# Eight vector additions and six rotation passes change engine, and one loop body is taken out of a TensorE loop

## The reference, cut to what matters

```python
hc = modulate(rms_norm_2(ctx, norm1_g[l]), m_ctx[0], m_ctx[1])   # needs sum(ctx*ctx) over 2048 features
...
qa = apply_rope(qa, cos_a, sin_a)     # x*cos + swapped(x)*sin
ka = apply_rope(ka, cos_a, sin_a)
qb = apply_rope(qb, cos_b, sin_b)
kb = apply_rope(kb, cos_b, sin_b)
...
merged = jax.nn.sigmoid(g_a) * (o_a @ w_br_a) + jax.nn.sigmoid(g_b) * (o_b @ w_br_b)
```

## Time and profile before

| | |
|---|---|
| median of 3 runs | 2875.73 us (2875.54 to 2875.75) |
| the profiled execution, its own time | 2876.91 us |
| its span in the trace | 2875.1 us |
| PE busy | 2811.4 us (98%) |
| DVE busy | 1997.1 us (69%) |
| ACT busy | 1274.9 us (44%) |
| POOL busy | 86.0 us (3%) |
| granted TensorE clock, mean | 0.994 |

### The profile page before, as it was taken

How to read it: one execution, slowest core, us unless ns; L and a number is a source line. 1 busy time by engine, 2 the same in 40 slices (tenths; PEclk the granted TensorE clock), 3 DMA queues, 4 the chain that set the end, 5 groups by cost and what they waited for, 6 DMA issues and landing times.

```text
span 2875.1 us, 52879 instructions
## 1 busy us (share of the span) xinstructions
PE 2811.4 (98%) x19046; PEld 2575.8 (90%) x19046; DVE 1997.1 (69%) x3060; ACT 1274.9 (44%) x1587; POOL 86.0 (3%) x74
## 2 busy tenths in 40 slices
PE   8998899999999999999999999999989999999999
PEld 8998899998899988888889898899988888888888
DVE  6776789867799987666678667866665555555554
ACT  5344455544454444211344455654444444344443
POOL 0011000100000000000003100000000000000000
PEclk9999999999999999999999999999999999999999
DMA  8874678667888885577777655666656666666665
GB/s 306 273 246 126 214 264 275 192 181 247 258 265 273 275 269 174 178 239 241 263 228 246 209 168 159 211 186 181 183 154 185 188 186 187 188 184 187 186 188 163
DMA packets 211744, 612.77 MB, mean 213 GB/s; under 512 B 23472, under 2 KB 31792, under 8 KB 210992
## 3 DMA queue, kind: packets, MB, share of 16 engines
q1 hardware_dynamic: 199296, 591.49, 65.9%
q10 hardware_dynamic: 11008, 14.60, 1.6%
q0 software_dynamic: 1328, 5.24, 0.5%
HBM read 600.75 MB, written 5.77 MB: 211 GB/s over the span
## 4 chain that ended last, share of the span: by engine, by line
PE 88%; DVE 6%; issue 3%; DMA 2%; ACT 1%; DVEq 0%; SPq 0%; ACTq 0%
PE acc L1624 24%; PE acc L1620 24%; PE acc L1622 12%; PE acc L1623 12%; DMA cond_rows<-w_ada 2%; PE acc L1608 2%; PE acc L1610 2%; PE acc L1611 2%; PE sums L1823 1%; PE acc L1618 1%; DVE cond_rows L1170 1%; PE acc L1831 1%; DVE wlo L1027 1%; PE turned L1816 1%; PE acc L1617 1%
## 5 line engine op out<-in xcount | busy, mean ns | idle before, releaser
L1027 DVE TENSOR_TENSOR wlo<-raw,whi 128x1024 fp32r<-128x1024 f32 x864 | 1064.2, 1233 | 713.9 <-ACT whi L560 711.5
L560 ACT ACTIVATE whi<-raw 128x1024 fp32r<-128x1024 f32 x864 | 914.6, 1060 | 1363.0 <-PE acc L1624 1132.4
L1624 PE MATMUL acc<-operand,wlo 128*128 128x256 f32 (+1 forms) x4816 | 1396.3, 290 | 0.0
L1622 PE MATMUL acc<-operand,whi 128*128 128x256 f32 (+1 forms) x3136 | 925.7, 295 | 29.2 <-DVE wlo L1027 14.0
L1624 PEld LDWEIGHTS acc<-operand,wlo 128*128 128x128 f32 x4816 | 921.8, 191 | 14.6
L1623 PE MATMUL acc<-operand,whi 128*128 128x256 f32 (+1 forms) x3136 | 923.9, 295 | 0.0
L1622 PEld LDWEIGHTS acc<-operand,whi 128*128 128x128 f32 x3136 | 603.4, 192 | 43.7 <-issue 25.4
L1623 PEld LDWEIGHTS acc<-operand,whi 128*128 128x128 f32 x3136 | 603.4, 192 | 12.7
L1620 PE MATMUL acc<-operand,whi 128*128 128x512 f32 x1680 | 599.9, 400 | 6.1 <-DVE operand L1385 5.7
L1620 PE MATMUL acc<-ffn_act,whi 128*128 128x512 f32 x1344 | 472.0, 395 | 0.0
L1620 PEld LDWEIGHTS acc<-operand,whi 128*128 128x128 f32 x1680 | 316.7, 189 | 81.7 <-issue 6.8
(11 more groups left out here) (220 smaller groups left out, 2005.2 us busy)
## 6 DMA issues: line engine op xcount, KB each, us to landing
cond_rows<-w_ada SPq DMA_DIRECT2D x512, 256.0 KB, 4.3
raw<-w_in SPq DMA_DIRECT2D x224, 512.0 KB, 3.6
raw<-w_up SPq DMA_DIRECT2D x176, 512.0 KB, 4.5
raw<-w_down SPq DMA_DIRECT2D x88, 512.0 KB, 3.7
raw<-w_fg SPq DMA_DIRECT2D x88, 512.0 KB, 3.8
raw<-w_fu SPq DMA_DIRECT2D x88, 512.0 KB, 3.5
raw<-w_fd SPq DMA_DIRECT2D x88, 512.0 KB, 3.5
raw<-w_o SPq DMA_DIRECT2D x32, 512.0 KB, 3.8
```

The source lines that it names most:

```text
L560: act.activation(whi[j % RING][:], raw[j % RING][:], ACT.Copy).then_inc(hi_done, 1)
L1027: dve.tensor_tensor(wlo[j % RING][:], raw[j % RING][:], whi[j % RING][:].bitcast(F32), ALU.subtract).then_inc(lo_done, 1)
L1622: pe.matmul(out_, h[:, x, f], mov[:, 0], start=first, stop=False)
L1624: ins = pe.matmul(out_, l[:, x, f], mov[:, 0], start=False, stop=last)
```

## The change

- GpSimd's 8 additions of the context squares are removed; VectorE gets the same 8 additions as `add_squares(i)`, put at steps 1, 2, 5 and 6 of the first two bodies of `up1b`. These two bodies are written out, the other three stay in VectorE's loop. ScalarE and TensorE keep their code there.
- GpSimd's 6 rotation passes for chunks 10 and 11 are removed; VectorE gets them one pass at a time, chunk 10 at steps 48, 50 and 52, chunk 11 at steps 58, 60 and 62, each after the norm work of the step and before the attention work of the step. The waits of those who read the chunks change accordingly.
- TensorE's first body of `branch_a` is written out, with the wait for one more group and the wait for the operand; the remaining three stay in a loop with `fresh=False`, and so without these two waits.

```diff
+        ctx_added = sem("context_squares_added")
...
-        TURNS_A = {6: 1, 0: 2, 7: 3, 1: 4, 8: 5, 9: 6}
-        TURNS_B = {2: 1, 3: 2, 4: 3, 5: 4, 10: 5, 11: 6}
+        TURNS_A = {6: 1, 0: 2, 7: 3, 1: 4, 8: 5, 9: 6, 10: 7, 11: 8}
+        TURNS_B = {2: 1, 3: 2, 4: 3, 5: 4}
+        TURN_AT = {48: (10, 0), 50: (10, 1), 52: (10, 2), 58: (11, 0), 60: (11, 1), 62: (11, 2)}
...
-            pool.wait_ge(sq_ready, SQ[5][0])
-            n, turn = KT // 2, 0
-            while n:
-                pool.wait_ge(poolstep, count)
-                for k in range(0, n, 2):
-                    pool.wait_ge(hi_done, unit(st_up1b, turn // st_up1b.upb, turn % st_up1b.upb) + 1)
-                    turn += 1
-                    a, b = (XC32[:, x + k:x + min(k + 2, n), 1, 1, :] for x in (0, n))
-                    step(pool.tensor_tensor(a, a, b, ALU.add))
-                n //= 2
-            pool.wait_ge(poolstep, count)
-            pool.sem_inc(acc_ready, 1)
...
-            for c in (2, 3, 4, 5, 10, 11):
+            for c in (2, 3, 4, 5):
                 for i in range(3):
                     rotate_late(c, i)
...
                         act.wait_ge(a_out, HA)
-                        act.wait_ge(n_late, 18)
+                        act.wait_ge(n_rope, 8)
...
-            run(st_up1b)
+            sums = [(n, k, min(k + 2, n)) for n in (8, 4, 2, 1) for k in range(0, n, 2)]
+
+            def add_squares(i):
+
+                n, k0, k1 = sums[i]
+                dve.wait_ge(sq_ready, SQ[5][0])
+                if n < 8:
+                    dve.wait_ge(ctx_added, [x[0] for x in sums].index(n))
+                dst, src = (XC32[:, x + k0:x + k1, 1, 1, :] for x in (0, n))
+                dve.tensor_tensor(dst, dst, src, ALU.add).then_inc(acc_ready if n == 1 else ctx_added, 1)
+
+            for b in range(2):
+                body(st_up1b, b, then={at: lambda i=4 * b + x: add_squares(i) for x, at in enumerate((1, 2, 5, 6))})
+            with dve.Fori(2, st_up1b.bodies) as b:
+                body(st_up1b, b)
...
-            def rotate(c):
+            def rotate(c, parts=range(3)):
 
                 n = TURNS_A[c]
                 chunk, sw, dims = rotation(c)
                 cos, sin = table(c)
-                if c < NK:
-                    dve.wait_ge(k_swap[c % 2], swapped(c))
-                else:
-                    dve.wait_ge(q_swap[c % 2], swapped(c))
-                    dve.wait_ge(n_sq, job_of[c] + 1)
-                    dve.wait_ge(n_table, 2)
-                dve.tensor_tensor(chunk, chunk, rep(cos, *dims), ALU.mult).then_inc(n_t1, 1)
-                dve.tensor_tensor(sw, sw, rep(sin, *dims), ALU.mult).then_inc(n_t2, 1)
-                dve.wait_ge(n_t1, n)
-                dve.wait_ge(n_t2, n)
-                dve.tensor_tensor(chunk, chunk, sw, ALU.add).then_inc(n_rope, 1)
+                if 0 in parts:
+                    if c < NK:
+                        dve.wait_ge(k_swap[c % 2], swapped(c))
+                    else:
+                        dve.wait_ge(q_swap[c % 2], swapped(c))
+                        dve.wait_ge(n_sq, job_of[c] + 1)
+                        dve.wait_ge(n_table, 4)
+                    dve.tensor_tensor(chunk, chunk, rep(cos, *dims), ALU.mult).then_inc(n_t1, 1)
+                if 1 in parts:
+                    dve.tensor_tensor(sw, sw, rep(sin, *dims), ALU.mult).then_inc(n_t2, 1)
+                if 2 in parts:
+                    dve.wait_ge(n_t1, n)
+                    dve.wait_ge(n_t2, n)
+                    dve.tensor_tensor(chunk, chunk, sw, ALU.add).then_inc(n_rope, 1)
...
-                    if c in TURNS_A and c >= NK:
+                    if c in TURNS_A and NK <= c < 10:
                         rotate(c)
+                if s in TURN_AT:
+                    rotate(TURN_AT[s][0], TURN_AT[s][1:])
...
                     if n == 0:
-                        pe.wait_ge(n_late, 18)
+                        pe.wait_ge(n_late, 12)
+                        pe.wait_ge(n_rope, 8)
                     score_b(n)
...
-            run(st_ba)
+            body(st_ba, 0)
+            with pe.Fori(1, st_ba.bodies) as b:
+                body(st_ba, b, fresh=False)
```

More of the change, by code:

```diff
@@ L535, in rotate_late @@
                 if step == 0:
-                    if c < NK:
-                        pool.wait_ge(k_swap[c % 2], swapped(c))
-                    else:
-                        pool.wait_ge(q_swap[c % 2], swapped(c))
-                        pool.wait_ge(n_sq, job_of[c] + 1)
+                    pool.wait_ge(k_swap[c % 2], swapped(c))
                     ins = pool.tensor_tensor(chunk, chunk, rep(cos, *dims), ALU.mult)
```

## The result

The changed kernel took 2856.97 us (median of 4 runs, 2856.56 to 2857.5) against 2875.74 us before. The ratio is 0.9932 with a 95% interval of 0.9919 to 0.9944. Times the 2875.73 us that the prediction started from, this is 2856.2 us. In a second session the same kernel came out at a ratio of 0.9941 (0.9926 to 0.9956), which is 2858.8 us by the same count. The prediction was 2858.4 us, with a range from 2856.8 to 2865.0.

A forecast was written before the change was run, and what follows sets the result against it. PE, busy for 98% of the span, bounds the kernel, so apart from the clock only its idle time can be won. Gains of 6.4+7.1+3.75 = 17.3 us from 2875.73 give 2858.4 us, range 2856.8 to 2865.

The forecast's parts named there:

- The squares: Near 534 us, moving GpSimd's additions to VectorE removes PE's 4.67 us idle time and 1.76 of slow clock and restart: 6.4 us.
- the slack of 2.0 us: Near 534 us, without GpSimd's additions VectorE's low part is done at 532.2, before PE asks at 534.20.
- The bound of 0.9 for the gain: Lower bound of the squares' gain, 0.9 us, against 5.5 us of additions on the path if VectorE's waits hid none.
- The rotations: Ahead of attention A, moving chunks 10 and 11 to VectorE gains 7.1 us of 8.3, bounds 1.2 and 8.3.
- the chain from the first exponential: Attention A: the 4.52 us from the first exponential to PE's transposes stay.
- the second wait of 0.4 us: After attention A's first transposes, a second small PE wait of 0.4 us can come, subtracted from the rotations' gain.
- the ring's bound: Before attention A's transposes, ScalarE's ring limits the start, leaving PE idle 0.1 to 0.3 us; 0.8 was taken.
- The cover for chunk 10's passes: At steps 48, 50 and 52 VectorE's DMA waits (2.38 us) hide the passes; 3.7 us without that cover.
- Rival (A): Wait ahead of attention A largely remains: chunk 10's passes add 3.7 us, idle 5.4, time 2864.4; chance 0.17.
- Branch A: Dropping the evacuation wait from three later bodies of the stage gains 3 x 1.25 = 3.75 us.
- the range's low end: Whole kernel: 2857.0 us in the likeliest case, all 18.5 us won; 2856.8 in the stated range.
- Rival (D): Attention steps 58 to 62: chunk 11's passes make PE wait in each step, costing 25 us, time 2883; chance 0.03.

The follow-up runs named there:

- the burst: Changed kernel with all eight square additions on VectorE in a row, ahead of the low part PE asks for after 534 us; ratio to the kernel before 0.9948.
- the experiment with whole rotations: Changed kernel with chunk 10's three passes together at step 46 and chunk 11's together at step 54; ratio to the kernel before 0.9945.
- the squares alone: Kernel before with only the context squares' additions moved from GpSimd to VectorE; ratio to the kernel before 0.998.
- the additions spread: Kernel before with the additions still on GpSimd, one for every second unit from the stage's second body on; ratio to the kernel before 0.9977.

## Why the prediction was right, and where it was not

**The squares** (6.4 us predicted, 6.43 measured): the step from 11.80 us on POOL to a late low part, and the slack of 2.0 us (2.3 by the burst), hold. The price of 0 for the additions holds for where they stand: the addition at 540.59 took 0.60 us of VectorE's idle time and PE shows no wait. The bound of 0.9 for the gain, with the cover gone, was close to what the burst left, 6.43-5.88 = 0.55 us.

**The rotations** (7.1 us predicted, 7.33 alone and 7.51 in the changed kernel): the chain from the first exponential (4.52 us before, 1587.97 to 1592.49 here) and the second wait of 0.4 us (0.39) came as worked out. The idle time that I took as 0.8 us was 0.37, near the ring's bound, and that is the mis-sized term of the sum: 8.34-0.37-0.39 = 7.6 us. Ahead of the first maximum VectorE waits for ScalarE and PE. In the 25 us ahead of the first exponential, all four profiles with chunk 10 on GpSimd have waits for `w_ada` DMAs as in the earlier trace rows, the longest of 1.96 to 2.39 us, and none has them with its passes in pieces on VectorE. So they were an after-effect of the stall by chunk 10 and no limit of their own. The cover for chunk 10's passes, which the prediction took from these DMA waits, came from waits for ScalarE instead (0.92 us at 1578.09). Rival (A) is out in the form in which it was priced, but the experiment with whole rotations shows its mechanism: passes ahead of the first maximum come onto the path in full.

**Branch A** (3.75 us predicted, 3.75 and 3.73 measured).

**Contention.** The rule of the Trainium skill, SBUF — State Buffer, "Who interferes with whom", agrees with the traces here where it says that the two engines lock each other out: VectorE's instructions are long beside GpSimd, and GpSimd's additions take up to 2.33 us beside VectorE. It also says what the prediction left out, that a VectorE instruction in a two-port mode contends with GpSimd too. The scaling passes of up to 1.24 us have one tensor as input, and so has a cast that takes 0.43 us elsewhere and 1.27 us beside a spread addition:

```profile
547.68 1.76 POOL L519 TENSOR_TENSOR operand_scratch<-operand_scratch 128x512 f32<-128x512 f32 x1 [3.43 <-ACT whi L560]
548.47 1.27 DVE L1153 CAST ffn_act<-conv_out 128x512 f32 x1 [0.17 <-DVE conv_out L1149]
```

**The step that failed** is the range's low end, "2857.0 (all 18.5 us won)" (2875.73-18.5 is 2857.2). It put every place that no edit touches at nothing. The prediction had read the granted clock as "1.00 elsewhere", and that was wrong: in the kernel before the clock is 0.91 in 203 to 213 us and 0.66 in 2120 to 2130. The changed places gave 6.43+7.51+3.75 = 17.7 us in the first profile, and the span fell by 20.3. Of the rest, 1.72 us lie before 245.96 and 1.15 in the 24 us after 2105 (0.2 come back later), in code that is the same, with a granted clock that differs between two profiles of one kernel. The low end should have been some 2 us lower for these places alone. The prediction's own figure for what a measurement can tell, 5.8 us, also stood against a low end 1.6 us below its centre. That the centre was met within 2.2 us by one session (19.5 us won) and 0.4 by the other (17.0) is in part luck, since nothing in the sum decides where these places fall. The statement that idle times of 1.88 us leave the clock alone was too strong as well: in the kernel with the squares alone the same wait, before 1874.18, had a body of 25.79 us behind it, with a granted clock of 0.84 from 1876 to 1886:

```profile
1876.00:1886.00 10.00, 10.00 (x74) 10.00 (x73) 5.87 (x4) 6.94 (x9) 0.00 (x0) 0.84 0.42 112
```

Rival (D) didn't come: the attention steps from 58 to 62 show no idle time, with 0.84 us to spare in the tightest one that I read.

**Open:** why the clock falls or not at the same idle time isn't settled. In the first block's attention it goes with the start of the stretch, but no run moved that start alone. Nor was it tried whether more of the 0.76 us left ahead of attention A can be had.

## What to carry to other kernels

A busy engine's idle time is a short list. Read it whole, and ask of each row what ran elsewhere at that time: the engine named as the releaser (VectorE here) may be slow only because a third one (GpSimd) works beside it. Work that is nobody's bottleneck is dear in one piece ahead of a result with little slack, on either engine. The squares' additions cost nothing in pieces behind the urgent low part, on VectorE or on GpSimd, and the same work in one burst ahead of it gave back 5.88 of 6.43 us; the rotations in whole gave back 5.94 of 7.51. Before a range is closed, look at the places that the edit doesn't touch: here they alone moved a profile by up to 1.7 us each. A first body that needs a stricter wait than the others belongs outside the loop, since in the loop each of the others pays for it.

## What the runs showed of the hardware that I had not expected

- An idle time of 2.95 us of PE cost 5.88 us in all, and one of 4.67 us cost 6.43: the slow clock behind the shorter wait took more. The idle time alone doesn't tell what a stall costs.
- Two profiles of one kernel have a granted clock of 1.00 and of 0.91 over the same 10 us, and the stretch of 43 to 45 us that they begin is 1.5 us longer in one.
- With the additions spread, GpSimd's addition of 128x512 took 2.23 to 2.34 us where it began beside a low part on VectorE, against a median of 1.40 for the eight in the kernel before, and four of VectorE's taps took 2.70 us instead of 1.67 beside one of them. Both sides pay, and VectorE lost 1.0 us in the taps to an instruction of 2.2.
